# Hybrid Hyena/MLA/GLA encoder on one core: the mixer's middle in another order, with the rope sum on VectorE

## What is computed

```python
x = x + 0.5 * swiglu_ffn(rms_norm(x, ffn1_norm), ...)
proj = rms_norm(x, mix_norm) @ w_in            # split into the branches' inputs
# Hyena: short convolution, then two long convolutions by FFT with gates
z = x1 * fft_long_conv(v, kern[:, 0], skip[0])
y = x2 * fft_long_conv(z, kern[:, 1], skip[1])          # then rms_norm
# MLA: latent attention, 4 heads, 128 plain and 64 rotary columns a head
q = cat(q_nope, rope(q_rope)); k = cat(k_nope, rope(k_rope))
o = softmax(q @ k.T * scale) @ v                        # then rms_norm
# GLA: gated linear attention, forward and backward, decay between all pairs of tokens
attn = einsum('bhid,bhjd,bhijd->bhij', qc, kc, decay); o = attn @ vc
x = x + concat([y_hy, y_mla, y_gla]) @ w_out
x = x + 0.5 * swiglu_ffn(rms_norm(x, ffn2_norm), ...)
```

## Time and profile before

| | us |
|---|---|
| median of 3 runs | 1030.52 |
| lowest and highest | 1030.11, 1030.55 |
| the profiled execution, its own time | 1030.28 |
| its span | 1028.3 |
| PE busy | 1001.0 (97%) |
| DVE busy | 694.3 (68%) |
| ACT busy | 537.3 (52%) |
| POOL busy | 110.9 (11%) |

### The profile page before, as it was taken

The page is one execution under the profiler, slowest core; times in us unless marked ns, Lnnn a source line. Parts: engine busy times, 40 slices in busy tenths (PEclk is TensorE's granted clock), DMA queues, the critical chain, the costliest instruction groups (busy, mean ns, idle before and its releaser), DMA issues.

```text
span 1028.3 us, 14899 instructions
## 1 busy us (share of the span) xinstructions
PE 1001.0 (97%) x5596; PEld 846.5 (82%) x5596; DVE 694.3 (68%) x826; ACT 537.3 (52%) x752; POOL 110.9 (11%) x160
## 2 busy tenths in 40 slices
PE   6999999999899999999999999999998999999997
PEld 5888888888777888888878888887886888888886
DVE  5766656676886666566677665657579776656665
ACT  6554545456654555454465454545466555545453
POOL 2000000150431200000020000003315220000001
PEclk9999999999999999999999999999999999999999
DMA  8466454444303564545455545452542235554551
GB/s 292 170 241 227 165 204 163 164 167 149 136 13 152 177 233 163 204 163 204 165 199 184 225 163 204 163 204 90 198 168 78 83 141 207 184 204 164 203 184 42
DMA packets 27080, 175.85 MB, mean 171 GB/s; under 512 B 3200, under 2 KB 3712, under 8 KB 6560
## 3 DMA queue, kind: packets, MB, share of 16 engines
q1 hardware_dynamic: 25744, 172.90, 45.8%
q0 software_dynamic: 720, 1.95, 0.8%
q10 hardware_dynamic: 576, 0.45, 0.1%
HBM read 174.58 MB, written 1.05 MB: 171 GB/s over the span
## 4 chain that ended last, share of the span: by engine, by line
issue 50%; PE 38%; POOL 9%; DVE 1%; DMA 1%; ACT 1%; POOLq 1%; SPq 0%; ACTq 0%; DVEq 0%
PE psum L1070 16%; PE psum L1071 8%; PE psum L1064 5%; PE psum L1066 4%; PE psum L1065 4%; POOL mixer_scratch L352 3%; POOL mixer_scratch L373 1%; POOL mixer_scratch L372 1%; DMA w_raw<-in_w_dram 1%; POOL statistics L325 1%; POOL statistics L323 1%; POOL x_normed L377 0%; POOL statistics L336 0%; ACT xT_split L430 0%; POOL statistics L339 0%
## 5 line engine op out<-in xcount | busy, mean ns | idle before, releaser
L1070 PE MATMUL psum<-xT_split,w_high 128*128 128x512 f32 x1408 | 501.6, 400 | 4.2 <-DVE w_low L702 2.4
L698 DVE TENSOR_TENSOR w_low<-w_raw,w_high 128x2048 fp32r<-128x2048 f32 (+1 forms) x160 | 362.8, 2270 | 134.4 <-ACT w_high L411 134.4
L1071 PE MATMUL psum<-xT_split,w_low 128*128 128x256 f32 x1408 | 395.6, 281 | 0.0
L1070 PEld LDWEIGHTS psum<-xT_split,w_high 128*128 128x128 f32 x1408 | 265.0, 188 | 72.9 <-issue 6.9
L411 ACT ACTIVATE w_high<-w_raw 128x2048 fp32r<-128x2048 f32 (+1 forms) x160 | 299.7, 1875 | 42.1 <-PE psum L1066 41.5
L1071 PEld LDWEIGHTS psum<-xT_split,w_low 128*128 128x128 f32 x1408 | 266.6, 189 | 1.4
L1064 PE MATMUL psum<-w_high,hT_high 128*128 128x512 f32 (+1 forms) x360 | 140.5, 390 | 0.0
L462 ACT ACTIVATE mixer_scratch<-psum 128x512 f32<-128x512 f32 x88 | 52.5, 596 | 167.4 <-PE psum L1071 167.4
L1066 PE MATMUL psum<-w_high,hT_low 128*128 128x512 f32 (+1 forms) x360 | 139.9, 389 | 0.0
L1065 PE MATMUL psum<-w_low,hT_high 128*128 128x512 f32 (+1 forms) x360 | 139.5, 387 | 0.0
L466 ACT ACTIVATE silu_gate<-hidden 128x256 f32<-128x256 f32 x88 | 36.8, 418 | 135.4 <-DVE hidden L727 135.4
(11 more groups left out here) (187 smaller groups left out, 989.3 us busy)
## 6 DMA issues: line engine op xcount, KB each, us to landing
w_raw<-in_w_dram SPq DMA_DIRECT2D x160, 1024.0 KB, 4.8
w_raw<-in_w_dram SPq DMA_DIRECT2D x8, 256.0 KB, 8.1
x<-in_x_dram SPq DMA_DIRECT2D x2, 512.0 KB, 5.2
mixer_scratch<-in_fil_dram POOLq DMA_DIRECT2D x2, 512.0 KB, 6.1
out_dram<-x_normed SPq DMA_DIRECT2D x3, 256.0 KB, 2.1
mixer_scratch<-in_fil_dram POOLq DMA_DIRECT2D x2, 352.0 KB, 6.1
mixer_scratch<-in_fin_dram SPq DMA_DIRECT2D x1, 512.0 KB, 5.4
dft<-in_dft_dram SPq DMA_DIRECT2D x1, 256.0 KB, 5.1
```

Of the source, the lines that this page charges most:

```text
L698: e.tensor_tensor(filled(WL[p], n), filled(raw[p], n), filled(WH[p], n).bitcast(F32), ALU.subtract).then_inc(s_lo.sem, 1)
L1070: e.matmul(out, ah, XB[:, k, :, :], start=k == 0, stop=False)
L1071: return e.matmul(out[:, 0:SEQ], al, XH[:, k, :], start=False, stop=k == KD - 1)
```

## The change

Only the mixer's middle is changed, in both layers alike. The set of instructions is the same but for one: the rope sum (an addition of two 128x512 tiles in SBUF) goes from POOL to DVE, right behind its products. The second value product goes into bank 0 in place of bank 6, behind `hy_dft(l, 1, 6)`. A helper `blocks_keep` is added and called by nothing. All else is order:

- POOL: `levels(l, 4)` ahead of the Hyena `rstd`.
- ACT: `level_exp` of rounds 0 to 3 earlier; the query copies ahead of the weight split of `S_WO`; the values behind keys and rotated query; `probs(l, 0)` ahead of the Hyena squares; the split of `S_WO + 1` and `S_WO + 2` later; `turned_high` of group 2 behind the split of `S_WO + 3`.
- DVE: `level_qk` of rounds 1 and 2 inside the first long convolution, `score_max(l, 0)` ahead of `level_keep(l, 0)`, the first `attended` later, `lo(l, S_WO + 2)` ahead of the GLA norm.
- PE: the first inverse ahead of the keys, the second `hy_dft` ahead of the second value product and the transposes of the rotated query, the scores in another order.

The diff, cut:

```diff
-                e.wait_ge(a_qt.sem, a_qt.at(l))
-                e.tensor_tensor(xn[:, :, 768:1024], PE_[:, 0:2, :], PE_[:, 2:4, :], ALU.add).then_inc(a_qr.sem, 1)
                 levels(l, 2)
                 levels(l, 3)
+                levels(l, 4)
                 rstd(l, h_sq, 2, T_SH, T_RH, I_H, 2, h_r)
-                levels(l, 4)
...
+                natural(l, 1, 2, 4)
                 hi(l, S_UQN)
-                natural(l, 1, 2, 4)
+                level_exp(l, 0)
                 natural(l, 2, 0, 7)
+                hi(l, S_UQR)
                 spectrum_odd(l, 0, 1)
-                hi(l, S_UQR)
-                level_exp(l, 0)
+                level_exp(l, 1)
+                level_exp(l, 2)
                 hi(l, S_UKV)
-                values_out(0)
                 natural(l, 3, 1, 4)
-                hi(l, S_WO)
-                values_out(1)
-                e.wait_ge(a_km.sem, a_km.at(l))
-                copy(KN[:, 0:2, :].rearrange("p a b -> p (a b)"), PS[:, 4, :], a_kn)
-                level_exp(l, 1)
                 e.wait_ge(s_used.sem, used(l, S_UQN))
                 for n in range(2):
                     copy(QN[:, 2 * n:2 * n + 2, :].rearrange("p a b -> p (a b)"), PS[:, 2 + n, :], a_qn)
+                hi(l, S_WO)
+                values_out(0)
+                values_out(1)
+                spectrum_odd(l, 1, 7)
+                level_exp(l, 3)
+                e.wait_ge(a_km.sem, a_km.at(l))
+                copy(KN[:, 0:2, :].rearrange("p a b -> p (a b)"), PS[:, 4, :], a_kn)
+                e.wait_ge(s_used.sem, used(l, S_UKV))
+                copy(KN[:, 2:4, :].rearrange("p a b -> p (a b)"), PS[:, 1, :], a_kn)
+                e.wait_ge(a_qtr.sem, a_qtr.at(l))
+                copy(QR.rearrange("p a b -> p (a b)"), PS[:, 2, :], a_qre)
                 e.wait_ge(a_vm.sem, a_vm.at(l))
                 copy(VM[:, 0, :], PS[:, 5, :], a_v)
-                copy(VM[:, 1, :], PS[:, 6, :], a_v)
-                e.wait_ge(a_qtr.sem, a_qtr.at(l))
-                copy(QR.rearrange("p a b -> p (a b)"), PS[:, 2, :], a_qre)
-                spectrum_odd(l, 1, 7)
-                hi(l, S_WO + 1)
-                e.wait_ge(s_used.sem, used(l, S_UKV))
-                copy(KN[:, 2:4, :].rearrange("p a b -> p (a b)"), PS[:, 1, :], a_kn)
-                level_exp(l, 2)
+                copy(VM[:, 1, :], PS[:, 0, :], a_v)
                 e.wait_ge(g_ls.sem, g_ls.at(l, 1))
                 copy(AD.rearrange("p h t c -> p h (t c)"), PS[:, 0:4, 0:256], g_la)
-                hi(l, S_WO + 2)
-                level_exp(l, 3)
+                hi(l, S_WO + 1)
+                level_exp(l, 4)
+                probs(l, 0)
                 e.wait_ge(h_z.sem, h_z.at(l, 2))
                 for t in range(T):
                     e.activation(TT[:, t, :], xn[:, t, 0:256], ACT.Square, accum_out=st[:, T_SH + t:T_SH + t + 1]).then_inc(h_sq.sem, 1)
-                level_exp(l, 4)
-                probs(l, 0)
                 level_exp(l, 5)
                 probs_turned(l, 0)
                 level_exp(l, 6)
@@ -664,16 +670,17 @@
                 turned_high(l, 2, 0, Y_BANKS[0], Y_TILES[0], C_GO, by_parity)
                 probs_turned(l, 1)
                 level_exp(l, 7)
+                hi(l, S_WO + 2)
                 attended_squares(0)
...
-                for n in range(4):
-                    taps(l, 3 + n, n, n, n)
-                lo(l, S_UQN)
-                join(l, 0, 0)
-                multiply(l, 0)
-                lo(l, S_UQR)
-                level_qk(l, 0)
-                lo(l, S_UKV)
-                combine(l)
-                fold(l)
-
-                e.wait_ge(s_used.sem, used(l, S_UQR))
...
+                taps(l, 3, 0, 0, 0); taps(l, 4, 1, 1, 1)
+                taps(l, 5, 2, 2, 2); taps(l, 6, 3, 3, 3)
+                lo(l, S_UQN)
+                level_qk(l, 0)
+                lo(l, S_UQR)
+                join(l, 0, 0)
+                level_qk(l, 1)
+                multiply(l, 0)
+                combine(l)
+                level_qk(l, 2)
+                fold(l)
+                lo(l, S_UKV)
+                e.wait_ge(s_used.sem, used(l, S_UQR))
                 e.tensor_tensor(t1, q, rp(0, 0, 64), ALU.mult)
                 e.tensor_tensor(t2[:, :, :, 0:32], q[:, :, :, 32:64], rp(1, 0, 32), ALU.mult)
                 e.tensor_tensor(t2[:, :, :, 32:64], q[:, :, :, 0:32], rp(1, 32, 64), ALU.mult).then_inc(a_qt.sem, 1)
+                e.wait_ge(a_qt.sem, a_qt.at(l))
+                e.tensor_tensor(xn[:, :, 768:1024], PE_[:, 0:2, :], PE_[:, 2:4, :], ALU.add).then_inc(a_qr.sem, 1)
                 gated(l, 0, 0)
                 lo(l, S_WO)
-                level_qk(l, 1)
                 join(l, 1, 6)
+                level_qk(l, 3)
                 multiply(l, 1)
                 combine(l)
                 fold(l)
-                level_qk(l, 2)
+                score_max(l, 0)
                 level_keep(l, 0)
                 gated(l, 1, 6)
-                level_qk(l, 3)
-                score_max(l, 0)
+                level_qk(l, 4)
                 level_keep(l, 1)
-                level_qk(l, 4)
+                level_qk(l, 5)
                 e.wait_ge(h_r.sem, h_r.at(l))
                 for t in range(T):
                     v = xn[:, t, 0:256]
                     r = e.tensor_scalar(v, v, st[:, T_RH + t:T_RH + t + 1], None, ALU.mult)
                 r.then_inc(h_yy.sem, 1)
                 level_keep(l, 2)
-                level_qk(l, 5)
                 score_max(l, 1)
                 level_keep(l, 3)
-                attended(l, 0)
+                level_qk(l, 6)
                 level_keep(l, 4)
                 turned_low(l, 2, 0, Y_BANKS[0], Y_TILES[0], C_GO, by_parity)
                 level_keep(l, 5)
-                level_qk(l, 6)
+                attended(l, 0)
                 attended(l, 1)
                 level_qk(l, 7)
                 level_keep(l, 6, 4)
...
                 lo(l, S_WO + 1)
-                for g in range(1, 3):
-                    turned_low(l, 2, g, Y_BANKS[g], Y_TILES[g], C_GO)
+                lo(l, S_WO + 2)
+                turned_low(l, 2, 1, Y_BANKS[1], Y_TILES[1], C_GO)
                 e.wait_ge(g_sq.sem, g_sq.at(l))
                 e.tensor_reduce(st[:, T_S8:T_S8 + 8], sg[:].rearrange("p t (h d) -> p (t h) d", d=GDV), AX.X, ALU.add).then_inc(g_s8.sem, 1)
-                lo(l, S_WO + 2)
...
+                turned_low(l, 2, 2, Y_BANKS[2], Y_TILES[2], C_GO)
                 turned_low(l, 2, 3, Y_BANKS[3], Y_TILES[3], C_GO)
...
-                e.wait_ge(g_az.sem, g_az.at(l))
+                def value(t, bank):
+                    p = pos(S_UKV)
+                    return passes(PS[:, bank, :], KVH[:, t * P:(t + 1) * P], KVL[:, t * P:(t + 1) * P], WH[p][:, 1, :], WL[p][:, 1, :], True, True)
...
+                hy_inverse(l, 0, 0).then_inc(h_inv.sem, 1)
                 e.wait_ge(s_lo.sem, s_lo.at(l, S_UKV + 1))
                 e.wait_ge(c_nat.sem, c_nat.at(l, 3))
...
-                for t in range(T):
-                    e.wait_ge(g_vr.sem, g_vr.at(l, t + 1))
-                    r = passes(PS[:, 5 + t, :], KVH[:, t * P:(t + 1) * P], KVL[:, t * P:(t + 1) * P], WH[p][:, 1, :], WL[p][:, 1, :], True, True)
-                r.then_inc(a_vm.sem, 1)
-                hy_inverse(l, 0, 0).then_inc(h_inv.sem, 1)
+                e.wait_ge(s_lo.sem, s_lo.at(l, S_UKV + 1))
+                e.wait_ge(g_vr.sem, g_vr.at(l, 1))
+                value(0, 5)
+                e.wait_ge(a_qt.sem, a_qt.at(l, 1))
+                e.wait_ge(g_vr.sem, g_vr.at(l, 2))
+                e.wait_ge(h_z.sem, h_z.at(l, 1))
+                hy_dft(l, 1, 6)
+                e.wait_ge(h_z.sem, h_z.at(l, 1))
+                value(1, 0).then_inc(a_vm.sem, 1)
+                e.wait_ge(s_lo.sem, s_lo.at(l, S_UKV + 1))
                 e.wait_ge(h_oc.sem, h_oc.at(l, 1))
                 keys((2, 3)).then_inc(s_used.sem, 1)
-                e.wait_ge(a_qr.sem, a_qr.at(l))
+                e.wait_ge(a_qr.sem, a_qr.at(l, 1))
                 e.wait_ge(a_qn.sem, a_qn.at(l, 2))
                 for pair in range(2):
                     for t in range(T):
                         r = e.transpose(PS[:, 2, pair * SEQ + t * P:pair * SEQ + (t + 1) * P], xn[:, t, 768 + pair * P:768 + (pair + 1) * P], ident)
                 r.then_inc(a_qtr.sem, 1)
+                e.wait_ge(s_kz.sem, 1)
+                e.wait_ge(a_qn.sem, a_qn.at(l, 2))
+                e.wait_ge(a_qre.sem, a_qre.at(l, 1))
+                e.wait_ge(a_kn.sem, a_kn.at(l, 1))
+                scores(l, 0, (0,))
+                e.wait_ge(a_kn.sem, a_kn.at(l, 2))
+                e.wait_ge(a_qre.sem, a_qre.at(l, 1))
                 e.wait_ge(a_v.sem, a_v.at(l, 2))
-                e.wait_ge(h_z.sem, h_z.at(l, 1))
-                hy_dft(l, 1, 6)
-                e.wait_ge(s_kz.sem, 1)
-                e.wait_ge(a_qre.sem, a_qre.at(l))
-                scores(l, 0, (0, 1))
```

(30 more changed lines are left out.)

46 lines of the change are left out of this document (28 added, 18 removed).

## The result

The changed kernel takes 1022.35 us, median of 4 runs (1022.07 to 1022.59), against 1030.42 of 4 runs before (1030.11 to 1030.55): a ratio of 0.9922, 95% interval 0.9910 to 0.9934, 8.1 us less. In a later set it took 1022.61 beside 1030.37 (0.9922). The profiled execution took 1022.59 with a span of 1020.8; before it was 1030.28 and 1028.3.

What follows compares the result with a forecast made beforehand. PE, busy for 97% of the span, bounds the kernel; only its mid-mixer waits can go. Terms of 3.6 and 0.2 a layer sum to 7.6 us, 5.5 with slower turns; 7.2 taken gives 1023.2 us, range 1020.8 to 1027.8.

Steps and rivals of the forecast that it cites:

- the walk: Step-by-step timing of the changed mixer middle from 266.32, giving 3.6 and 0.2 us a layer, 7.6 us in all.
- The first convolution: On DVE, with POOL's levels 1 and 2 inside it: `fold` ends at 265.65, PE's first inverse starts without a wait.
- The turns: DVE and POOL alternating in the first long convolution: 0.32 us for each POOL addition between two DVE operations.
- the slow ones: Each DVE and POOL turn 0.1 us longer: `fold` at 266.6, second `hy_dft` at 270.8, gain 5.5 us.
- Rope sum: The sum takes 0.6 us on DVE against 1.22 on POOL; PE's 1.11 wait ahead of the transposes goes.
- values: ACT's four value copies end at 269.5; the second `hy_dft` starts at 269.8 instead of 272.66.
- the new wait: PE waits 0.8 us for ACT's copy of `QR` ahead of the first scores, which start at 274.45.
- The second convolution: DVE's `fold` ends at 278.6 instead of 281.9; second inverse at 280.5 without its 1.55 wait; round 1 at 282.65.
- The rounds: PE's steps from round 1 sum to 18.0, with waits of 0.7 at round 5 and 0.25 at round 7; lead 3.6.
- The tail: Earlier split of `S_WO + 2` shortens POOL's first GLA `rstd` step; the 0.22 wait ahead of `turn_group` 3 goes.
- (a): Rival: the rounds keep DVE's pace, 19.17 us from round 1 to round 7; gain 1.24 and 0.2 a layer, 1027.5; chance 0.15.
- (c): Rival: first convolution hangs on POOL's level chain; levels 0 and 1 taking 14 us give 1034.3, slower; chance 0.07.

Runs made afterwards that it cites:

- The tail alone: The kernel before with only DVE's split of `S_WO + 2` moved ahead of the GLA norm: 1029.29 us, ratio 0.9992.

## Why the prediction was right

The forecast was 1023.2 against 1022.35, a gain of 7.2 against 8.1 (7.5 by the spans). Point by point, with 0.16 taken off the trace's times: that execution came by so much later to the first inverse, from which the walk starts (266.48 against 266.32), without having waited there.

- *The first convolution.* `fold` was walked to 265.65 and ended at 265.68 in the trace's own time, 265.52 with the 0.16 off; the inverse started without a wait. The turns were those of the walk and not the slow ones: the second `hy_dft` is at 269.66, against 269.8 walked and 270.8 for slow turns. Level 1 took 4.13 beside `level_qk` and `multiply`, where it had taken 2.06, and `multiply` 1.54 and 1.42, by 0.2 to 0.3 more than the 1.22 of before. The rule of the Trainium skill (SBUF — State Buffer, Who interferes with whom) fits this trace: the two `join`s of the second convolution, each with one input in PSUM, took 0.69 and 0.68 beside POOL's level 3, as they had with POOL idle, and `multiply` and `fold`, with both inputs in SBUF, grew beside the levels.
- *Rope sum, values, the new wait.* All as walked: 0.94 instead of 0.8 ahead of the scores, which start at 274.41 (274.45 walked). That the sum's new engine is not what gains was not in the prediction. The kernel with it late on POOL shows that.
- *The second convolution and round 1.* The second inverse is at 280.51 (280.5 walked), round 1 at 282.71 (282.65).
- *The rounds.* The turn of the attention output comes at 301.85, walked to 301.6; the wait at round 5 is 0.61 (0.7 walked). So the lead at the turn is 3.36, where the sum had 3.6.
- *The tail.* Here the term was too small: 0.2 stood in the sum, and from the turn to `turn_group` 3 it is 11.31 instead of 11.68, 0.37. The tail alone on the kernel before gives 0.40. What was missed is the part of the wait hidden behind a modelled end, which was counted elsewhere but not here.

The walk's sum, 3.8 a layer, met 3.7, and that close in part by luck: the lead was 0.24 too large and the tail 0.17 too small. Taking 7.2 instead of 7.6 for it, out of caution, moved the forecast away from the result. Of the rivals, (a) did not come: from round 1 to round 7 it is 16.99 instead of 19.17. (c) names a real mechanism, with its place: one addition more on POOL spends the slack. Its price was too low. It had the losses begin at 8.3 us for levels 0 and 1 together, and the gain gone at 12.1. They take 7.0 in the changed kernel and, with what the additions put in between, 8.5 with one and 11.0 with three. At 8.5 `hy_dft` was already 1.26 late where (c) gives 0.2, and at 11.0 `gated` was 3.80 late where (c) gives 2.7. So the slack is about 0.2 and not 1.3, and the gain is gone at about 11, the fallen clock not counted.

What stays open: which moves make up the rest of the gain. Of 3.7 a layer the rope sum alone gave 1.0, the tail alone 0.4, and the second value product in its old bank and place took 1.2 away; the early levels, the order of the keys and that of the scores were not tried alone, and the parts need not add up. Open too are the 0.6 us between the gain by the set's medians (8.1; 7.8 in the later set) and by the marks (7.5). The granted clock of the first 20 us differs from one execution to the next. The kernel before may also lose clock in some: of its 27 runs in one set three had a mean granted clock of 0.995 and took 1031.18 to 1031.41, where the median is 1030.33. Its traced execution shows no fall in either mixer, so nothing here says where those three lost it.
